# Chunk products of an mLSTM as three products of high and low parts, split by three engines

## The chip, the cores and the metric

One core of a Trainium2 chip runs the whole kernel. The metric is the device time of one execution in microseconds (us); lower is better. The core has TensorE (PE, matrix products; PEld are its weight loads), VectorE (DVE), ScalarE (ACT), GpSimd (POOL) and SyncE (SP), which issues the transfers. Each takes its own instructions in order and waits on semaphores.

## The reference

A layer over 1024 tokens of width 1024: one wide projection `h @ w_in`, an mLSTM branch, a dilated window attention branch, and an output projection. The change touches the mLSTM branch: 4 heads, head width 256, 8 chunks of 128 tokens (L = 128). For each head and chunk n:

```
C_new = decay * C + einsum('l,lk,lv->kv', w, k_j, v_j)          # the state, 256 x 256
n_new = decay * n + einsum('l,lk->k', w, k_j)
s     = einsum('ld,sd->ls', q, k) * exp(log_d - m_t)            # 128 x 128
num   = inter * einsum('ld,dv->lv', q, C_prev) + einsum('ls,sv->lv', s, v)
den   = inter * (q @ n_prev) + s.sum(-1)
h     = num / maximum(|den|, exp(-m_t))
```

A column of ones appended to v gives n and den in the same products (width VE = 258, two such columns).

## The kernel before, in words

The big projections run on TensorE as a list of products by Strassen-like blocks. One product (a **step**, numbered k) is 12 matmuls of 128 x 512: four k-tiles times three passes, (high weight, high data), (high weight, low data), (low weight, high data), all in the type fp32r, in which one matmul is one pass. The high part is a copy rounded to fp32r, the low part is what is left. For the weights of step k+3 ScalarE makes the high part at its step k (L1456, `high`, which waits until product k-1 is done, so that a ring place is free), and then GpSimd (L1080) or, for the products called P7 and P3, VectorE (L1887) subtracts it to get the low part (`low`). GpSimd also makes the weight sums S1 and S2 (L1068, L1074) once in seven steps, S2 after a `low` of VectorE.

Everything else is side work, written into lists per step: `items[k]` are done by TensorE ahead of product k and by the other engines at their step k; `act_late`, `dve_late`, `pool_late`, `sp_late` come last in an engine's step k. In its step GpSimd first makes `low(k+3)` (if it is its own), then the sums, then `pool_late`. ScalarE takes results out, then `high(k+3)`, then `act_late`.

The 32 chunks (c = 8h + n) are placed by hand in `start_of`: head 0 starts at steps 177, 180, 183, 186, 190, 193, 196, 199, head 1 from 203 and head 2 from 238 with 4 or 5 steps between chunks, head 3 at 273, 276, 280, 283, 287, 290, 294, 297.

- `start` at step s: TensorE makes the scores (L1317) and turns o, k and v (L1321, L1332, L1334). ScalarE copies v and scaled k out of PSUM (L1721, L1723), takes the exponential (L1726) and the output gate (L1730). VectorE makes `w` = scores x exponentials (L2165).
- `end` at step s+2: TensorE makes A = q x state (L1345, two matmuls 128 x 258, none for n = 0), B = w x v (L1350, one), C = k x v (L1354, two, none for n = 7), all in fp32 (four passes, which the profile shows as two records for each matmul). ScalarE copies B (L1738), VectorE adds A (L2172), divides, and brings the state up to date (L2190).
- The square of the chunk's output (L1656) is at ScalarE's step s+3. SyncE fetches chunk c+2 into the buffer of chunk c (`chunk_in`) at the step of `end` of c.

VectorE also has the taps of the convolution in head 0 to 2's stretch (L2001, 128 x 1021 to 1023, both inputs in SBUF), one at one step and two at the next, and the silu after them (L2011).

Of the kernel before, what the change touches and what calls it, by code (L numbers as in the profile page):

```python
# [13 lines left out]
P = 128  # L14
# [27 lines left out]
HM_SLOTS = 12  # L42
# [103 lines left out]
def hybrid_kernel(nc, x, w_in, w_if, w_pm, w_pa, w_out, b_gate, conv_wt, conv_bt, pre_wt, m_wt, post_w,  # L146
# [240 lines left out]
    def chunk_no(h, n):  # L387
        return NT * h + n
# [10 lines left out]
    with ctx:  # L399
# [65 lines left out]
        hm_sb = at("hm_sb", [P, HM_SLOTS, MD], F32, A_Q)  # L465
# [15 lines left out]
        sq_junk = small("sq_junk", [P, MD], BF16, 2)  # L481
# [47 lines left out]
        ifw = small("ifw", [P, KT, 2 * MH], F32)  # L529
        assert pos[0] <= nc.sbuf_usable_end, (pos[0], nc.sbuf_usable_end)  # L530
# [51 lines left out]
        x2_in = [sem(f"x2_in{i}") for i in range(4)]  # L582
# [9 lines left out]
        x_sq = sem("x_sq")  # L592
# [13 lines left out]
        e_done, kv_done, sq_done = sem("e_done"), sem("kv_done"), sem("sq_done")  # L606
        m_norm = sem("m_norm")
        att_hi, hm_hi, w_out_hi = sem("att_hi"), sem("hm_hi"), sem("w_out_hi")
        ysq_done, mg_hi = sem("ysq_done"), sem("mg_hi")

        v_step = sem("v_step")
        x_ms, x_sq_late, x_scaled = sem("x_ms"), sem("x_sq_late"), sem("x_scaled")
# [11 lines left out]
        d_done, s34_done, lo_dve = sem("d_done"), sem("s34_done"), sem("lo_dve")  # L624
        a_used, chunk_ready, ones_done = sem("a_used"), sem("chunk_ready"), sem("ones_done")
        m_ms, m_fac = sem("m_ms"), sem("m_fac")
# [3 lines left out]
        y_ms, y_read, y_done = sem("y_ms"), sem("y_read"), sem("y_done")  # L630

        g_ready = sem("g_ready")
        x_rs, x_norm = sem("x_rs"), sem("x_norm")
        s12_done = sem("s12_done")
        lo_pool = sem("lo_pool")
        m_rs, y_rs = sem("m_rs"), sem("y_rs")
# [1674 lines left out]
```

## Time and profile before

| | |
|---|---|
| median of 3 runs | 1371.04 us (1370.8 to 1371.63) |
| the profiled execution, its time | 1369.94 us |
| its span from first to last instruction | 1368.1 us |
| mean granted TensorE clock | 0.998 |
| busy share PE, PEld, DVE, ACT, POOL | 99%, 82%, 58%, 47%, 42% |

The span is what the views of the trace divide up; the profiled execution's time lies 1.84 us above it, and 1.10 us below the median of the runs.

### The profile page before, as it was taken

Reading aid. Unit: us, or ns where it says so; the run is one execution under the profiler, and the core shown is the slowest. Engines: PE = TensorE matmul, PEld = TensorE weight load, DVE = VectorE, ACT = ScalarE, POOL = GpSimd, SP = SyncE. Lnnn points to the kernel's source line nnn. Section 1 sums busy time; section 2 is a strip of 40 time slices with the busy share of each in tenths; the row PEclk is TensorE's granted clock in tenths of the full one; section 3 lists DMA queues with packets and bytes.
Section 4 is the critical chain, followed back from the end, with each engine's and each line's share of the span. In section 5 each row is a group of like instructions: output and inputs, shape, how many; then the busy total and the mean of one; then the engine's idle time right before and its main releaser. Section 6 shows DMA issues by size and latency. Waiting matters only on the chain.

```text
span 1368.1 us, 18779 instructions
## 1 busy us (share of the span) xinstructions
PE 1352.3 (99%) x6470; PEld 1127.3 (82%) x6470; DVE 794.5 (58%) x1260; ACT 641.7 (47%) x1320; POOL 569.2 (42%) x400
## 2 busy tenths in 40 slices
PE   7999999999999999999999999999999999999998
PEld 5788888888888888888888888888888888888786
DVE  5874438346543835877756575755644442997632
ACT  6644543543444455345445445544544553533421
POOL 5253435335443534654434445344333544454000
PEclk9999999999999999999999999999999999999999
DMA  6132233324233323455442634345343354966421
GB/s 194 51 76 65 69 74 90 96 48 126 76 85 72 84 79 61 149 173 144 114 145 66 188 104 134 100 127 175 87 150 97 93 188 165 345 200 196 183 97 58
DMA packets 210462, 165.02 MB, mean 121 GB/s; under 512 B 32400, under 2 KB 186544, under 8 KB 210368
## 3 DMA queue, kind: packets, MB, share of 16 engines
q1 hardware_dynamic: 210224, 163.75, 40.5%
q8 instruction: 53, 0.87, 0.3%
q14 instruction: 41, 0.34, 0.1%
q10 hardware_dynamic: 144, 0.07, 0.0%
HBM read 117.41 MB, written 40.08 MB: 115 GB/s over the span
## 4 chain that ended last, share of the span: by engine, by line
PE 91%; DVE 4%; issue 2%; ACT 1%; DMA 1%; SPq 1%; POOL 0%; DVEq 0%; POOLq 0%; ACTq 0%
PE proj L1244 69%; PE side L1189 3%; PE proj L1189 2%; PE side L1289 2%; PE side L1268 2%; PE side L1345 2%; PE side L1354 2%; PE proj L1170 2%; PE side L1170 2%; PE side L1277 1%; PE side L1317 1%; PE side L1350 1%; PE side L1300 1%; DMA x_sb<-x_in 1%; PE side L1362 1%
## 5 line engine op out<-in xcount | busy, mean ns | idle before, releaser
L1080 POOL TENSOR_TENSOR w_lo<-raw,w_hi 128x512 fp32r<-128x512 f32 x161 | 234.5, 1458 | 413.8 <-ACT w_hi L1456 413.7
L1244 PE MATMUL proj<-hi_T,w_hi 128*128 128x512 f32 x832 | 338.1, 406 | 2.2 <-ACT snap L1474 1.6
L1244 PE MATMUL proj<-hi_T,w_lo 128*128 128x512 f32 x832 | 325.2, 391 | 0.0
L1244 PE MATMUL proj<-lo_T,w_hi 128*128 128x512 f32 x832 | 324.1, 390 | 0.0
L1244 PE MATMUL proj<-hi_B,w_hi 128*128 128x512 f32 x624 | 254.1, 407 | 5.6 <-ACT b_sb L1518 4.0
L1244 PE MATMUL proj<-hi_B,w_lo 128*128 128x512 f32 x624 | 244.2, 391 | 0.0
L1244 PE MATMUL proj<-lo_B,w_hi 128*128 128x512 f32 x624 | 243.6, 390 | 0.0
L1080 POOL TENSOR_TENSOR w_lo<-s_sb,w_hi 128x512 fp32r<-128x512 f32 x104 | 156.7, 1510 | 153.5 <-ACT w_hi L1456 153.4
L1244 PEld LDWEIGHTS proj<-hi_T,w_hi 128*128 128x128 f32 x832 | 156.4, 188 | 36.0 <-issue 3.5
L1244 PEld LDWEIGHTS proj<-hi_T,w_lo 128*128 128x128 f32 x832 | 156.1, 188 | 34.2
L1244 PEld LDWEIGHTS proj<-lo_T,w_hi 128*128 128x128 f32 x832 | 156.6, 188 | 30.4
L1456 ACT ACTIVATE w_hi<-raw 128x512 fp32r<-128x512 f32 x216 | 135.2, 627 | 70.5 <-PE proj L1244 57.6
L1244 PEld LDWEIGHTS proj<-hi_B,w_hi 128*128 128x128 f32 x624 | 117.7, 189 | 29.9 <-ACT b_sb L1518 4.2
L1244 PEld LDWEIGHTS proj<-hi_B,w_lo 128*128 128x128 f32 x624 | 117.4, 188 | 25.4
L1244 PEld LDWEIGHTS proj<-lo_B,w_hi 128*128 128x128 f32 x624 | 117.8, 189 | 22.8
L1074 POOL TENSOR_TENSOR s_sb<-s_sb,raw 128x512 f32<-128x512 f32 x52 | 82.9, 1594 | 91.3 <-DVE w_lo L1887 90.5
L1456 ACT ACTIVATE w_hi<-s_sb 128x512 fp32r<-128x512 f32 x156 | 97.7, 627 | 37.9 <-PE proj L1244 28.9
L1887 DVE TENSOR_TENSOR w_lo<-s_sb,w_hi 128x512 fp32r<-128x512 f32 x52 | 43.9, 845 | 85.5 <-ACT w_hi L1456 85.5
L1068 POOL TENSOR_TENSOR s_sb<-raw 128x512 f32<-128x512 f32 x52 | 75.5, 1453 | 21.5 <-DVE w_lo L1887 21.4
L2001 DVE SCALAR_TENSOR_TENSOR tmp<-stage,cw,tmp 128x1023 f32<-128x1023 f32 (+2 forms) x48 | 76.1, 1585 | 0.7
L2144 DVE CUSTOM_DVE_ANT_0 prob<-side,mask_sb 128x128 f32<-128x128 f32 (+1 forms) x96 | 29.2, 347 | 67.3 <-PE side L1268 67.2
L1474 ACT ACTIVATE snap<-proj 128x512 f32<-128x512 f32 x52 | 31.1, 597 | 78.0 <-PE proj L1244 77.9
(253 smaller groups left out, 2014.5 us busy)
## 6 DMA issues: line engine op xcount, KB each, us to landing
raw<-w_in SPq DMA_DIRECT2D x95, 512.0 KB, 6.0
m_spill<-stage SPq DMA_DIRECT2D x16, 1024.0 KB, 5.6
chunk<-m_spill SPq DMA_DIRECT2D x32, 512.0 KB, 3.8
gate_spill<-stage SPq DMA_DIRECT2D x8, 1024.0 KB, 4.3
gst<-gate_spill SPq DMA_DIRECT2D x32, 256.0 KB, 3.2
share<-share_spill SPq DMA_DIRECT2D x12, 512.0 KB, 5.0
x_sb<-x_in SPq DMA_DIRECT2D x8, 512.0 KB, 7.6
hm_spill<-stage SPq DMA_DIRECT2D x4, 1024.0 KB, 8.8
```

Of the source, the lines that this page charges most:

```text
L1068: ins = TT(s1_sb[:], a21, a22, ALU.add)
L1074: ins = TT(s2_sb[:], s1_sb[:], a11, ALU.subtract)
L1080: TT(w_lo_ring[k % RING][:], src, w_hi_ring[k % RING][:].bitcast(F32), ALU.subtract).then_inc(lo_pool, 1)
L1170: mm = pe.matmul(pa_slot(t)[:, tokens], w[:, kt, :], m[:, kt, tokens], start=(kt == 0 and w is wh and m is at_hi), stop=(kt == AH - 1 and ...
L1189: mm = pe.matmul(y_slot(t)[:, columns], a[:, kt, :], w[i][:, j, columns], start=(kt == 0 and a is hi_part and w is out_hi), stop=(kt == KT ...
L1244: mm = pe.matmul(acc(p, which), w[:, kt, :], m[:, kt, :], start=(first and kt == 0 and w is wh and m is h_hi[b]), stop=(kt == 3 and w is w ...
L1268: mm = pe.matmul(b[:, at_ * P:(at_ + m) * P], qo_sb[(NG * h + g) % 4][:, n * P:(n + 1) * P], k_sb[g][:, (n + 1 - m) * P:(n + 1) * P], star ...
L1456: A(w_hi_ring[k % RING][:], src, ACT.Copy).then_inc(hi_done, 1)
L1474: A(snap[0][:], a, ACT.Copy).then_inc(u3_done, 1)
L1887: TT(w_lo_ring[k % RING][:], operand(p, weight_name(k)), w_hi_ring[k % RING][:].bitcast(F32), ALU.subtract).then_inc(lo_dve, 1)
L2001: ins = STT(t_[:, d:], src[:, 0:S - d], cw[:, t, 3 - d:4 - d], t_[:, d:], ALU.mult, ALU.add)
L2144: ins = V.tensor_tensor_reduce(out=prob_part(h, i)[:, part], in0=b[:, part], in1=mask, scale=-ASCALE, scalar=3.0e38, op0=ALU.add, op1=ALU. ...
```

## The change

All of A, B and C go from fp32 to three fp32r products of high and low parts; the scores stay fp32. The parts are made so:

- q: high by ScalarE as the first thing of `start` (128 x 256), low by GpSimd in `pool_late[s]` (in place over q in the chunk's buffer, so it also waits until the scores are made).
- k, v: high by ScalarE (the two copies that were there, with fp32r outputs), low by VectorE, two more operations that read PSUM (128 x 256 each), between `dmat` and `w`.
- w: VectorE writes it over the exponentials, ScalarE makes the high part in `act_late[s+1]` (128 x 128), GpSimd the low part in `pool_late[s+1]`.
- state: high by ScalarE in `act_late[e+1]`, low by GpSimd in `pool_late[e+1]` (128 x 516 each), e being the step of `end`.

`end` is at e = s+2 where the next chunk starts by s+3 (head 0: n = 0, 1, 2, 4, 5, 6; head 3: n = 0, 2, 4, 6) and at e = s+3 elsewhere. Single buffers take the place of double ones for k, v, w and the output gate; the outputs' ring has 10 places for 12; some semaphores are merged to make room.

```diff
-HM_SLOTS = 12
+HM_SLOTS = 10
...
+    end_of = {}
+    for c, at_ in enumerate(chunks):
+        s = start_of[at_]
+        end_of[at_] = s + (2 if c + 1 < len(chunks) and start_of[chunks[c + 1]] <= s + 3 else 3)
     for h, n in chunks:
-        s = start_of[h, n]
+        s, e = start_of[h, n], end_of[h, n]
         c = NT * h + n
         ready = 7 * pair_of["mo", h] + (10 if h else 11)
-        free = start_of[chunks[c - 2]] + 2 if c > 1 else 171
+        free = end_of[chunks[c - 2]] if c > 1 else 171
         sp_late[max(free, ready)].append(("chunk_in", h, n))
         items[s].append(("start", h, n))
-        items[s + 2].append(("end", h, n))
-        act_late[s + 3].append(("square", h, n))
+        items[e].append(("end", h, n))
+        act_late[s + 1].append(("w_high", h, n))
+        if n:
+            pool_late[s].append(("q_low", h, n))
+        pool_late[s + 1].append(("w_low", h, n))
+        act_late[e + 1].append(("square", h, n))
+        if n < NT - 1:
+            act_late[e + 1].append(("state_high", h, n))
+            pool_late[e + 1].append(("state", h, n))
...
         state = small("state", [P, 2, VE], F32)
-        kw_sb = [small(f"kw{i}", [P, MD], F32) for i in range(2)]
-        vv_sb = [small(f"vv{i}", [P, VE], F32) for i in range(2)]
-        w_sb = [small(f"w{i}", [P, P], F32) for i in range(2)]
-        o_gate = [small(f"o_gate{i}", [P, MD], F32) for i in range(2)]
-        dmat = small("dmat", [P, P], F32)
+        state_hi = small("state_hi", [P, 2, VE], F32R)
+        state_lo = at("state_lo", [P, 2, VE], F32R, A_P + 26112)
+        q_hi = small("q_hi", [P, 2, P], F32R)
+        q_lo = [at(f"q_lo{i}", [P, 2, P], F32R, A_P + 16896 + i * 4608) for i in range(2)]
+        kw_hi, kw_lo = small("kw_hi", [P, MD], F32R), small("kw_lo", [P, MD], F32R)
+        vv_hi, vv_lo = small("vv_hi", [P, VE], F32R), small("vv_lo", [P, VE], F32R)
+        cw_hi, cw_lo = small("cw_hi", [P, P], F32R), small("cw_lo", [P, P], F32R)
+        o_gate = small("o_gate", [P, MD], F32)
+        dmat = at("dmat", [P, P], F32, A_P + 26112 + 2112)
...
+                    if what == "q_low":
+                        h, n = it[1:]
+                        c = chunk_no(h, n)
+                        g.wait_ge(q_high, later_no(h, n))
+                        g.wait_ge(pe_ring, ring_no["qk", h, n] + 1)
+                        TT(q_lo[c % 2][:], chunk_sb[c % 2][:, 0:2, :], q_hi[:].bitcast(F32), ALU.subtract
+                           ).then_inc(q_low, 1)
+                    elif what == "w_low":
+                        h, n = it[1:]
+                        g.wait_ge(w_high, chunk_no(h, n) + 1)
+                        TT(cw_lo[:], dmat[:], cw_hi[:].bitcast(F32), ALU.subtract).then_inc(w_done, 1)
+                    elif what == "state":
+                        h, n = it[1:]
+                        g.wait_ge(state_high, (NT - 1) * h + n + 1)
+                        TT(state_lo[:], state[:], state_hi[:].bitcast(F32), ALU.subtract).then_inc(state_done, 1)
...
+            def three_products(into, w, m):
+
+                for i, (a, b) in enumerate(((0, 0), (0, 1), (1, 0))):
+                    mm = pe.matmul(into, w[a], m[b], start=(i == 0), stop=(i == 2))
+                return mm
+
             def chunk_end(h, n):
                 c = chunk_no(h, n)
-                v = vv_sb[c % 2][:]
+                v = (vv_hi[:], vv_lo[:])
                 pe.wait_ge(kv_done, c + 1)
                 pe.wait_ge(ones_done, 1)
                 if n:
-                    ring_taken(pe, ("C", h, n - 1, 1))
+                    pe.wait_ge(q_low, later_no(h, n))
+                    pe.wait_ge(state_done, later_no(h, n))
                     for d in range(2):
-                        mm = pe.matmul(keep[:, 0:VE], chunk_sb[c % 2][:, d, :], state[:, d, :],
-                                       start=(d == 0), stop=(d == 1))
+                        for a, m in ((q_hi, state_hi), (q_hi, state_lo), (q_lo[c % 2], state_hi)):
+                            mm = pe.matmul(keep[:, 0:VE], a[:, d, :], m[:, d, :],
+                                           start=(d == 0 and a is q_hi and m is state_hi), stop=(d == 1 and a is not q_hi))
                     mm.then_inc(pe_keep, 1)
-                ring_taken(pe, ("qk", h, n))
+                pe.wait_ge(w_done, c + 1)
                 b = work(("B", h, n))
-                pe.matmul(b[:, 0:VE], w_sb[c % 2][:], v, start=True, stop=True).then_inc(pe_ring, 1)
+                three_products(b[:, 0:VE], (cw_hi[:], cw_lo[:]), v).then_inc(pe_ring, 1)
                 if n < NT - 1:
                     for d in range(2):
                         b = work(("C", h, n, d))
-                        pe.matmul(b[:, 0:VE], kw_sb[c % 2][:, d * P:(d + 1) * P], v, start=True, stop=True
-                                  ).then_inc(pe_ring, 1)
+                        keys = slice(d * P, (d + 1) * P)
+                        three_products(b[:, 0:VE], (kw_hi[:, keys], kw_lo[:, keys]), v).then_inc(pe_ring, 1)
...
+                elif what == "w_high":
+                    h, n = it[1:]
+                    c = chunk_no(h, n)
+                    ring_taken(act, ("qk", h, n))
+                    if c:
+                        act.wait_ge(pe_ring, ring_no["B", *divmod(c - 1, NT)] + 1)
+                    A(cw_hi[:], dmat[:], ACT.Copy).then_inc(w_high, 1)
+                elif what == "state_high":
+                    h, n = it[1:]
+                    ring_taken(act, ("C", h, n, 1))
+                    if n:
+                        act.wait_ge(pe_keep, keep_no["A", h, n] + 1)
+                    elif h:
+                        act.wait_ge(pe_keep, keep_no["A", h - 1, NT - 1] + 1)
+                    A(state_hi[:], state[:], ACT.Copy).then_inc(state_high, 1)
...
+                        if n:
+
+                            if later_no(h, n) > 1:
+                                hp, n2 = (h, n - 1) if n > 1 else (h - 1, NT - 1)
+                                act.wait_ge(pe_keep, keep_no["A", hp, n2] + 1)
+                            act.wait_ge(chunk_in[c % 2], 32 * (c // 2 + 1))
+                            A(q_hi[:], chunk_sb[c % 2][:, 0:2, :], ACT.Copy).then_inc(q_high, 1)
                         act.wait_ge(pe_keep, keep_no["kv", h, n] + 1)
-                        if c > 1:
-                            act.wait_ge(pe_ring, ring_no[last_use(*divmod(c - 2, NT))] + 1)
-                        ins = A(vv_sb[c % 2][:, 0:MD], keep[:, MD:2 * MD], ACT.Copy)
+                        if c:
+                            act.wait_ge(pe_ring, ring_no[last_use(*divmod(c - 1, NT))] + 1)
+                        ins = A(vv_hi[:, 0:MD], keep[:, MD:2 * MD], ACT.Copy)
                         if n < NT - 1:
-                            ins = A(kw_sb[c % 2][:], keep[:, 0:MD], ACT.Copy, scale=cols[:, 2, h, n:n + 1])
-                        ins.then_inc(kv_done, 1)
+                            ins = A(kw_hi[:], keep[:, 0:MD], ACT.Copy, scale=cols[:, 2, h, n:n + 1])
+                        ins.then_inc(kv_hi, 1)
                         act.wait_ge(d_done, c + 1)
                         A(dmat[:], dmat[:], ACT.Exp, bias=cols[:, 0, h, n:n + 1]).then_inc(e_done, 1)
                         act.wait_ge(pe_ring, ring_no["oT", h, n] + 1)
-                        if c > 1:
-                            act.wait_ge(chunk_ready, c - 1)
-                        A(o_gate[c % 2][:], bank[ring_no["oT", h, n] % BANKS][:, 0:MD], ACT.Tanh, scale=0.5
+                        if c:
+                            act.wait_ge(chunk_ready, c)
+                        A(o_gate[:], bank[ring_no["oT", h, n] % BANKS][:, 0:MD], ACT.Tanh, scale=0.5
                           ).then_inc(ring_act, 1)
...
+                dve.wait_ge(kv_hi, c + 1)
+                ins = TT(vv_lo[:, 0:MD], keep[:, MD:2 * MD], vv_hi[:, 0:MD].bitcast(F32), ALU.subtract)
+                if n < NT - 1:
+                    ins = STT(kw_lo[:], keep[:, 0:MD], cols[:, 2, h, n:n + 1], kw_hi[:].bitcast(F32), ALU.mult, ALU.subtract)
+                ins.then_inc(kv_done, 1)
                 i = ring_no["qk", h, n]
                 dve.wait_ge(pe_ring, i + 1)
-                if c > 1:
-                    dve.wait_ge(pe_ring, ring_no["B", (c - 2) // NT, (c - 2) % NT] + 1)
                 dve.wait_ge(e_done, c + 1)
-                TT(w_sb[c % 2][:], bank[i % BANKS][:, 0:P], dmat[:], ALU.mult).then_inc(ring_dve, 1)
+                TT(dmat[:], bank[i % BANKS][:, 0:P], dmat[:], ALU.mult).then_inc(ring_dve, 1)
...
+                    if chunk_no(h, n) - h:
+                        dve.wait_ge(state_done, chunk_no(h, n) - h)
```

## Rows read from the trace of the kernel before

**Rows 1.** One window: PE, PEld, DVE, ACT, POOL busy; clock; DMA share; GB/s

```profile
612.00:700.00 88.00, 88.00 (x430) 74.52 (x429) 62.45 (x105) 44.04 (x96) 35.56 (x24) 1.00 0.43 126
```

**Rows 2.** Groups of PE by form: times records, busy us, mean ns

```profile
L1244 PE MATMUL proj<-hi_T,w_lo 128*128 128x512 f32 x832 | 325.2, 391 | 0.0
...
L1354 PE MATMUL side<-vv,kw 128*128 128x258 f32 x112 | 28.9, 381 | 0.0
L1345 PE MATMUL side<-state,chunk 128*128 128x258 f32 x112 | 28.9, 379 | 0.0
...
L1350 PE MATMUL side<-vv,w 128*128 128x258 f32 x64 | 19.1, 379 | 0.0
```

**Rows 3.** The chain in order of time: start, us, what

```profile
619.84 0.43 PE side L1350 x2
...
623.89 0.44 PE side L1317 x4
...
624.99 5.47 PE proj L1244 x24
630.46 0.87 PE side L1345 x4
631.33 0.43 PE side L1350 x2
```

**Rows 4.** Weight loads: scores (ns min/median/max), projection (busy, mean ns, idle)

```profile
L1317 PEld LDWEIGHTS side<-chunk x128: 187/190/192, 612.9 to 1042.4; 128*128 128x128 f32 x128
...
L1244 PEld LDWEIGHTS proj<-hi_T,w_lo 128*128 128x128 f32 x832 | 156.1, 188 | 34.2
```

**Rows 5.** Groups by form of POOL, ACT and DVE

```profile
L1080 POOL TENSOR_TENSOR w_lo<-raw,w_hi 128x512 fp32r<-128x512 f32 x161 | 234.5, 1458 | 413.8 <-ACT w_hi L1456 413.7
...
L1456 ACT ACTIVATE w_hi<-raw 128x512 fp32r<-128x512 f32 x72 | 45.2, 628 | 19.2 <-PE proj L1244 19.2
...
L1721 ACT ACTIVATE vv<-side 128x256 f32<-128x256 f32 x32 | 12.3, 384 | 34.2 <-PE side L1334 34.2
...
L2172 DVE SCALAR_TENSOR_TENSOR total<-side,cols,total 128x258 f32<-128x258 f32 x28 | 13.6, 485 | 26.1 <-ACT total L1738 25.8
```

**Rows 6.** Timeline of POOL: start, us, what [idle before it]

```profile
616.40 4.09 POOL L1080 TENSOR_TENSOR w_lo<-raw,w_hi 128x512 fp32r<-128x512 f32 x2 [6.04 <-ACT w_hi L1456]
...
627.63 1.87 POOL L1080 TENSOR_TENSOR w_lo<-raw,w_hi 128x512 fp32r<-128x512 f32 x1 [2.06 <-ACT w_hi L1456]
629.46 2.25 POOL L1080 TENSOR_TENSOR w_lo<-s_sb,w_hi 128x512 fp32r<-128x512 f32 x1
...
665.80 1.39 POOL L1080 TENSOR_TENSOR w_lo<-raw,w_hi 128x512 fp32r<-128x512 f32 x1 [4.85 <-ACT w_hi L1456]
...
678.61 1.72 POOL L1080 TENSOR_TENSOR w_lo<-raw,w_hi 128x512 fp32r<-128x512 f32 x1
...
688.05 1.30 POOL L1080 TENSOR_TENSOR w_lo<-s_sb,w_hi 128x512 fp32r<-128x512 f32 x1 [5.21 <-ACT w_hi L1456]
...
1008.15 1.29 POOL L1080 TENSOR_TENSOR w_lo<-s_sb,w_hi 128x512 fp32r<-128x512 f32 x1 [3.24 <-ACT w_hi L1456]
```

**Rows 7.** Timeline of DVE and ACT beside it

```profile
627.07 5.72 DVE L2001 SCALAR_TENSOR_TENSOR tmp<-stage,cw,tmp 128x1023 f32<-128x1023 f32 x3
...
663.48 0.64 ACT L1456 ACTIVATE w_hi<-raw 128x512 fp32r<-128x512 f32 x1
```

**Rows 8.** The chain where PE reaches the ends of later chunks

```profile
667.72 0.87 PE side L1345 x4
...
679.23 0.87 PE side L1345 x4
...
690.74 0.87 PE side L1345 x4
...
1011.68 0.87 PE side L1345 x4
```

**Rows 9.** DMA issues of the page: KB each, us to landing

```profile
chunk<-m_spill SPq DMA_DIRECT2D x32, 512.0 KB, 3.8
```

More of the change, by code:

```diff
@@ L581, in hybrid_kernel @@
         out_in = [sem(f"out_in{i}") for i in range(4)]
-        x2_in = [sem(f"x2_in{i}") for i in range(4)]
         y_out = [sem(f"y_out{i}") for i in range(4)]
@@ L590, in hybrid_kernel @@
         pe_y = sem("pe_y")
-        x_sq = sem("x_sq")
+        row_sq = sem("row_sq")
         b1_hi = sem("b1_hi")
@@ L1127, in _ @@
                     what = it[0]
-                    if what == "norm":
+                    if what == "q_low":
[13 more added lines that the diff above has]
+                        TT(state_lo[:], state[:], state_hi[:].bitcast(F32), ALU.subtract).then_inc(state_done, 1)
+                    elif what == "norm":
                         h = it[1]
-                        g.wait_ge(m_ms, h + 1)
-                        TT(mrs[:], msq[:, h % 2], halfneg[:], ALU.pow).then_inc(m_rs, 1)
+                        g.wait_ge(mean_sq, MS_M + h + 1)
+                        TT(mrs[:], msq[:, h % 2], halfneg[:], ALU.pow).then_inc(root, 1)
             for t in range(NT):
-                g.wait_ge(y_ms, t + 1)
-                TT(yrs[:, t:t + 1], ysum[:, t:t + 1], halfneg[:, 0:1], ALU.pow).then_inc(y_rs, 1)
+                g.wait_ge(mean_sq, MS_Y + t + 1)
+                TT(yrs[:, t:t + 1], ysum[:, t:t + 1], halfneg[:, 0:1], ALU.pow).then_inc(root, 1)
         @block.tensor
@@ L1499, in y_squares @@
                 if t or half:
-                    act.wait_ge(ysq_done, 2 * t + half)
+                    act.wait_ge(row_sq, SQ_Y + 2 * t + half)
                 A(y_junk[:], y_slot(t)[:, half_of(half)], ACT.Square, scale=DM ** -0.5,
-                  accum_out=ysq[:, t, half:half + 1]).then_inc(ysq_done, 1)
+                  accum_out=ysq[:, t, half:half + 1]).then_inc(row_sq, 1)
             def square(t):
@@ L2020, in piece @@
                         dve.wait_ge(sq_done, NT * (h + 1))
-                        TS(msq[:, h % 2], msq[:, h % 2], 1.0 / MD, 4.0 * EPS, ALU.mult, ALU.add).then_inc(m_ms, 1)
+                        TS(msq[:, h % 2], msq[:, h % 2], 1.0 / MD, 4.0 * EPS, ALU.mult, ALU.add).then_inc(mean_sq, 1)
                     else:
-                        dve.wait_ge(m_rs, h + 1)
+                        dve.wait_ge(root, ROOT_M + h + 1)
                         TT(mfac[:], mrs[:], rden[:, h % 2], ALU.mult).then_inc(m_fac, 1)
@@ L2039, in mean_square @@
             def mean_square(t):
-                dve.wait_ge(x_sq, t + 1)
-                TS(ssq[:, t:t + 1], ssq[:, t:t + 1], EPS, None, ALU.add).then_inc(x_ms, 1)
+                dve.wait_ge(row_sq, t + 1)
+                TS(ssq[:, t:t + 1], ssq[:, t:t + 1], EPS, None, ALU.add).then_inc(mean_sq, 1)
             def first_low(kt):
@@ L2182, in chunk_end @@
                     dve.wait_ge(pe_ring, ring_no["hmT", hp, 2 + n2 // 4] + 1)
-                STT(hm_slot(h, n), o_gate[c % 2][:], 1.0, total[:, 0:MD], ALU.add, ALU.mult).then_inc(chunk_ready, 1)
+                STT(hm_slot(h, n), o_gate[:], 1.0, total[:, 0:MD], ALU.add, ALU.mult).then_inc(chunk_ready, 1)
                 if n < NT - 1:
+                    if chunk_no(h, n) - h:
+                        dve.wait_ge(state_done, chunk_no(h, n) - h)
                     for d in range(2):
@@ L2231, in result @@
                     columns = half_of(half)
-                    dve.wait_ge(ysq_done, 2 * t + half + 1)
+                    dve.wait_ge(row_sq, SQ_Y + 2 * t + half + 1)
                     if half:
-                        STT(ysum[:, t:t + 1], ysq[:, t, 0:1], EPS, ysq[:, t, 1:2], ALU.add, ALU.add).then_inc(y_ms, 1)
+                        STT(ysum[:, t:t + 1], ysq[:, t, 0:1], EPS, ysq[:, t, 1:2], ALU.add, ALU.add).then_inc(mean_sq, 1)
                     elif t == 0:
@@ L2241, in result @@
                 dve.wait_ge(y_read, 2 * t + 2)
-                dve.wait_ge(y_rs, t + 1)
-                dve.wait_ge(x2_in[t % 4], 16 * (t // 4 + 1))
+                dve.wait_ge(root, ROOT_Y + t + 1)
+                dve.wait_ge(x_in[t], 32)
                 parts = [slice(0, DM)] if t < NT - 1 else [half_of(0), half_of(1)]
```

41 lines of the change are left out of this document (22 added, 19 removed).

## The prediction

> **What bounds the kernel now.** I read first the windows over the stretch of the chunks. From 612 to 700 us TensorE is busy for 88.00 of 88.00 us at a granted clock of 1.00, its higher level of 2.4 GHz, while GpSimd is busy for 35.56 us [rows 1]. The chain that ended last says the same: in this stretch it is TensorE's own instructions, one behind the other [rows 3]. So each microsecond taken off TensorE in it is a microsecond off the time, and each microsecond that TensorE newly waits is one on top; there is no slack to spend. The groups by form then give what is replaced, the chain its pace, and the timelines of GpSimd, VectorE and ScalarE show how early the inputs of `end` could be ready.
>
> **What TensorE saves.** The groups hold 112 records for C, 112 for A and 64 for B [rows 2], two for each matmul: 56 + 56 + 32 = 144 matmuls of 128 x 258. In the chain two of them take 0.87 us [rows 3], 0.435 us each, 62.6 us in all. Each becomes three matmuls of one pass, a form that the trace does not have at this width. Bounds from the nearest rows:
> - From below: a record of the scores is two passes over 128 columns with a weight load of its own, and four of them take 0.44 us [rows 3], 0.110 us. So a weight load and 256 column-times fit into 0.110 us, and the loads of fp32 and of the fp32r products have the same 188 to 190 ns [rows 4]. 258 columns in one pass then take no less than 0.110: 144 x (0.435 - 0.330) = 15.1 us saved.
> - From above: 24 fp32r matmuls of 512 columns take 5.47 us [rows 3], 0.228 each, where 512 columns at 2.4 GHz are 0.213 and the fp32 record of 2 x 258 columns, 0.2175, lies only 0.0025 over its 0.215. fp32r has some 0.0125 us more. If that is a fixed price, a matmul takes 0.1225: 144 x (0.435 - 0.3675) = 9.7 us.
> - If it goes with the columns, 0.0025 stays and the rest of 0.228 is scaled: 0.0025 + 258/512 x 0.2255 = 0.116, so 144 x (0.435 - 0.348) = 12.5 us. I take this one, between the two.
>
> The Trainium skill (TensorE: Matmul & The Clock Gate, section Back-to-back issue gap) has N/2.4 + 2.5 ns for a matmul at the high clock, 110 ns here, by which the saving would be 15.1 us. For 512 columns it gives 216 ns where this trace has 228, so I don't go by it.
>
> **What is added to the others.** GpSimd: a low part of 512 columns takes 1.29 to 1.30 us alone [rows 6] and 1.46 in the mean [rows 5]. By columns the state's low part is 1.30, the queries' 0.65 and w's 0.35 (estimates), up to 2.30 us per chunk, some 66 us in all. GpSimd's 35.56 busy us of 88 [rows 1] have room for it; the order is the question. ScalarE: a 512 copy is 0.63 and a 256 one 0.38 [rows 5], so q's high part 0.38, w's about 0.3, state's 0.63: 1.3 us per chunk, in an engine half idle; q's comes while it waited for `start` anyway. VectorE: two reads of PSUM of 256 columns, about 0.43 each by half to all of the 0.485 for 258 columns [rows 5]: 0.86 us, between `dmat` and `w`, of which about half falls into its wait for ScalarE's exponential (an estimate). Were that cover gone, it would be 0.86 later with its taps; products wait for VectorE's results only two steps (5.5 us) later. The fetch of chunk c+2, moved with `end`, has three or more steps (over 8 us) to land in 3.8 [rows 9]: no price; SyncE's queue behind it waits for nothing new but `end` itself. Merged semaphores, the ring of 10 and single buffers: their last users are a step or more before, no price. Where `end` moves to s+3 the same work stands one product later: nothing.
>
> **Where TensorE will wait.** `end` needs the low parts of q and state (for A) and of w (for B), all from GpSimd, which serves strictly in order: at step s low(s+3), state, q; at step s+1 low(s+4), w. TensorE needs them after `start` and two products, 6.57 us after s. A itself takes six passes, 0.70 us, before w is needed. In the six tight chunks of head 0 that is not enough. I add to the end of GpSimd's last old instruction what now stands in its queue:
> - chunk 0 (no A): GpSimd ended both lows at 620.49 [rows 6], w's part ends at 620.84, B was due at 619.84 [rows 3]: 1.0 us.
> - chunk 1: the second low ended at 631.71 [rows 6]; with 1.30 + 0.65 + 0.35 it is 634.0; B was due at 630.46 [rows 3] + 0.70 = 631.16: 2.85 us.
> - chunk 4 (and chunk 2, with the same distances): ScalarE's high part ends at 664.12 [rows 7], then square and the state's high part until 665.3; 1.30 + 0.65 + 1.29 + 0.35 give 668.9, B due at 667.72 [rows 8] + 0.70: 0.5 us each.
> - chunk 5: low(197), behind the sums, ended at 680.33 [rows 6]; 682.63 against 679.23 [rows 8] + 0.70: 2.7 us.
> - chunk 6: low(199) ended at 689.35 [rows 6], then 1.95 until q's part, against A at 690.74 [rows 8]: 0.6 us.
>
> That is 8.2 us, the lower end. It leaves out what VectorE does to GpSimd. Alone a low takes 1.29; beside three taps of VectorE the two lows took 1.87 and 2.25, and the three taps, back to back in VectorE's program, 5.72 us [rows 6, 7]. The 1.54 us that GpSimd lost and the ends of both fit only one order: tap, low, tap, low, tap, each about 1.1 us and each alone. So an added GpSimd instruction beside an operation of VectorE that reads two SBUF tiles lets one such operation in ahead of it. Replayed so: chunk 1 runs low 628.6 to 629.9, tap, state 631.0 to 632.3, tap, q until 634.1, low 635.4, w 635.8: A waits 3.6 and B 0.9 more, 4.5 us. Likewise chunk 4 gets two taps more (3.6), chunk 5 one tap and a sum (4.2), chunk 6 a sum of 0.6, a low and the silu (2.7), chunk 2 a silu (1.2), chunk 0 sometimes a tap (1.4). Sum 17.6 us.
>
> The Trainium skill (SBUF — State Buffer, section Who interferes with whom) says that a VectorE instruction with two SBUF inputs and a GpSimd instruction that reads SBUF exclude each other for the whole instruction, in order of issue. Were it only the mean of the lows, 1.46 for 1.29, the added queue would wait 13% longer and the stalls stay near 10 us; by the rule they are near the 17.6. The pair 1.87 and 2.25 is on its side.
>
> Elsewhere there is little: in head 3 VectorE has no taps, low(290) ends at 1009.44 [rows 6], state, q and w need 2.30, and A comes at 1011.68 [rows 8]; nothing to 0.3. With `end` at s+3 GpSimd has 2.75 us more. Only where the two sums (2.6 us) fall in between as well (chunk 1 of heads 1 and 2) up to 0.8 us each. I take 0.5 us for all of these, bounds 0 and 1.6.
>
> **Sum.** -12.5 + 17.6 + 0.5 = +5.6 us: 1369.94 would become 1375.5 in the profiled execution, and on the median of the runs, 1371.04 + 5.6 = 1376.6 us. A measurement of this kernel can tell about 0.2%, 2.7 us.
>
> **Rivals.**
> 1. Faster: VectorE and GpSimd hardly block each other, as GpSimd takes its turns in the silent places of VectorE. For it: the lows of 1.29 outside the taps [rows 6]. Against: the pair in chunk 1. Stalls 8.2, saving 12.5 to 15.1: 1371.04 less 4.3 to 6.9, so 1364 to 1367. It decides when the stalls are under 12.5 - 2.7 = 9.8 us.
> 2. The waits spread: ScalarE, which gates GpSimd's lows, is itself late (it waits in order for B, for the taps and for the gate's buffer, now single), and chunks at s+3 wait too. At 0.5 us in each of 20 other chunks that is 10 us more: 1387.
> 3. The change doesn't do what it says: narrow one-pass matmuls don't run at their width. If each took the 0.228 of a 512 one, 144 x (0.684 - 0.435) = 36 us come on top, 1425 with the stalls; at 0.145 nothing is saved, 1389. Against it the 0.110 of the scores' records.
>
> **Chances.** Forecast's case 0.56 (in it 0.40 slower, 0.16 within 0.2%, for its stalls of 13 to 20 us and saving of 9.7 to 15.1 make 1369 to 1382); rival 1 0.27 (0.20 faster, 0.07 same); rival 2 0.11; rival 3 0.06. Faster 0.20, same 0.23, slower 0.57. The range from 1364 (8.2 us of stalls against 15.1) to 1385 leaves out most of rivals 2 and 3 and a little of rival 1.
>
> **What the profile after would show.** Records of A, B, C 432 in number, 0.33 to 0.37 us of the chain for three; TensorE idle for the first time between 612 and 700 us, most of it released by GpSimd's low parts of q, state and w, in head 0's chunks 1, 4, 5 and 6, none in head 3; the state's low part about 1.3 us alone and above 2 beside taps; TensorE's side work shorter by 12.5 us. Wrong makes me: GpSimd's narrow operations cheaper or dearer than their columns, an order of turns other than one by one, or a pace of the narrow matmuls off 0.116.

## The result, and the profile after

The changed kernel takes 1396.42 us in the median of 4 runs (1394.99 to 1397.56), the kernel before 1370.92 beside it (4 runs, 1369.49 to 1371.63): 1.0188 times as long, interval 1.0176 to 1.0200, or 25.5 us slower. Slower was the forecast, 1376.6 us was not: the time lies outside the range of 1364 to 1385. The profiled execution took 1396.55 us; its span is 1394.7 us where before it was 1368.1, and its mean granted clock 0.991 where it was 0.998.

The busy times on the page of the changed kernel, engine by engine (us, share of the span, instructions):

```profile
PE 1356.0 (97%) x6614; PEld 1131.7 (81%) x6614; DVE 835.7 (60%) x1320; ACT 671.5 (48%) x1408; POOL 671.9 (48%) x488
```

No share looks alarming. The window over the first 88 us of the chunks, in the columns of [rows 1], does:

```profile
612.00:700.00 88.00, 75.41 (x370) 62.95 (x369) 54.94 (x95) 40.96 (x93) 48.08 (x35) 0.92 0.37 103
```

TensorE, which had no idle time here, now idles for 12.59 us, and its clock is 0.92 of full speed. The waits of TensorE (what for, us in total, times, longest) name the cause of the idle time:

```profile
PE side L1377 <- POOL cw_lo L1160: 13.0, 14, 1.7
PE side L1390 <- POOL q_lo L1155: 8.7, 8, 3.3
PE proj L1281 <- ACT b_sb L1563: 5.0, 1, 5.0
```

The first two are new, 21.7 us in 22 places; the third is a wait near the kernel's start (at 18 us), 4.0 us long before. It changes from kernel to kernel (2.8 to 5.4 us in those below), which the comparisons of spans carry with them. Where in chunks 1, 4 and 5 of head 0 they fall, TensorE's timeline shows (start, us, what, idle before it):

```profile
633.05 0.39 PE L1281 MATMUL proj<-hi_T,w_lo 128*128 128x512 f32 x1
636.74 0.36 PE L1390 MATMUL side<-state_hi,q_hi 128*128 128x258 f32 x1 [3.30 <-POOL q_lo L1155]
638.18 0.39 PE L1377 MATMUL side<-vv_hi,cw_hi 128*128 128x258 f32 x1 [0.49 <-POOL cw_lo L1160]
...
678.16 0.36 PE L1390 MATMUL side<-state_hi,q_hi 128*128 128x258 f32 x1 [1.41 <-POOL q_lo L1155]
680.58 0.58 PE L1377 MATMUL side<-vv_hi,cw_hi 128*128 128x258 f32 x1 [1.45 <-POOL cw_lo L1160]
...
696.02 0.36 PE L1390 MATMUL side<-state_hi,q_hi 128*128 128x258 f32 x1 [2.04 <-POOL q_lo L1155]
698.43 0.58 PE L1377 MATMUL side<-vv_hi,cw_hi 128*128 128x258 f32 x1 [1.38 <-POOL cw_lo L1160]
```

The same 128 x 258 matmul is written with 0.39 us at 638.18 and with 0.58 at 680.58 and 698.43. That is the clock. Windows of TensorE alone (us, PE busy, PEclk, DMA share, GB/s), first three short ones at the waits, then three of 25 us that hold them:

```profile
638.00:642.00 4.00, 3.81 (x15) 0.59 0.51 150
680.00:686.00 6.00, 5.42 (x17) 0.50 0.35 98
697.00:703.00 6.00, 4.62 (x16) 0.50 0.34 98
625.00:650.00 25.00, 21.21 (x103) 0.93 0.36 97
675.00:700.00 25.00, 18.72 (x82) 0.80 0.31 83
700.00:725.00 25.00, 24.54 (x119) 0.93 0.37 122
```

In each of the three places the granted clock is at its lower level of 1.2 GHz (0.50) for 3 to 7 us. It does not fall at the same point of each: at 638.8 us, 0.6 us after the second wait of chunk 1; at 679.7, inside the second wait of chunk 4; and at 696.8, after the 2.04 us ahead of chunk 5's A and before the wait for w began. Before, this stretch ran at 1.00 [rows 1]. The three windows of 25 us give 25 x (0.07 + 0.20 + 0.07) = 8.5 us of lost clock, but in chunks 4 and 5 a part of it passed while TensorE stood idle. What was lost in work is read from the starts of the matmuls (the first two follow each other at the lower clock, 0.43 us apart, the last two at the higher, 0.25 apart; a narrow product takes 0.215 and not 0.12):

```profile
685.66 0.63 PE L1281 MATMUL proj<-lo_T,w_hi 128*128 128x512 f32 x1
686.09 0.60 PE L1281 MATMUL proj<-hi_T,w_lo 128*128 128x512 f32 x1
686.52 0.41 PE L1281 MATMUL proj<-hi_T,w_hi 128*128 128x512 f32 x1
686.77 0.40 PE L1281 MATMUL proj<-lo_T,w_hi 128*128 128x512 f32 x1
```

Over the three places the matmuls at the lower clock take 6.6 us more than at the higher: 4.3 in 22 projection products, 2.0 in 21 narrow ones, 0.3 in the two first ones behind a wait.

GpSimd's added work, by form (columns as in [rows 5]), is dearer than forecast:

```profile
L1164 POOL TENSOR_TENSOR state_lo<-state,state_hi 128x516 fp32r<-128x516 f32 x28 | 41.3, 1473 | 23.4 <-ACT state_hi L1709 23.4
L1155 POOL TENSOR_TENSOR q_lo<-chunk,q_hi 128x256 fp32r<-128x256 f32 x28 | 35.7, 1275 | 0.0
L1160 POOL TENSOR_TENSOR cw_lo<-dmat,cw_hi 128x128 fp32r<-128x128 f32 x32 | 22.1, 691 | 1.5 <-ACT cw_hi L1701 1.5
```

They take 99.1 us in all, where 66 were estimated; the queries' part has a mean of 1.28 us and not 0.65, w's 0.69 and not 0.35. A little of it is the narrow operations themselves: the shortest take 0.73 and 0.44 us. Chunk 1 shows where the most comes from. GpSimd's timeline there:

```profile
630.65 1.96 POOL L1102 TENSOR_TENSOR w_lo<-raw,w_hi 128x512 fp32r<-128x512 f32 x1 [2.06 <-ACT w_hi L1501]
632.57 2.25 POOL L1164 TENSOR_TENSOR state_lo<-state,state_hi 128x516 fp32r<-128x516 f32 x1
634.78 1.70 POOL L1155 TENSOR_TENSOR q_lo<-chunk,q_hi 128x256 fp32r<-128x256 f32 x1
636.45 1.27 POOL L1102 TENSOR_TENSOR w_lo<-s_sb,w_hi 128x512 fp32r<-128x512 f32 x1
637.68 0.45 POOL L1160 TENSOR_TENSOR cw_lo<-dmat,cw_hi 128x128 fp32r<-128x128 f32 x1
...
827.00 1.96 POOL L1102 TENSOR_TENSOR w_lo<-raw,w_hi 128x512 fp32r<-128x512 f32 x1 [2.06 <-ACT w_hi L1501]
828.92 1.73 POOL L1155 TENSOR_TENSOR q_lo<-chunk,q_hi 128x256 fp32r<-128x256 f32 x1
830.61 2.26 POOL L1102 TENSOR_TENSOR w_lo<-s_sb,w_hi 128x512 fp32r<-128x512 f32 x1
832.82 0.45 POOL L1160 TENSOR_TENSOR cw_lo<-dmat,cw_hi 128x128 fp32r<-128x128 f32 x1
```

and VectorE's beside its first three lines:

```profile
630.18 5.71 DVE L2068 SCALAR_TENSOR_TENSOR tmp<-stage,cw,tmp 128x1023 f32<-128x1023 f32 x3
```

While the three taps run, each GpSimd instruction is longer than alone, by 0.69, 0.95 and 0.97 us: 1.96, 2.25 and 1.70 us for a weight's low part, the state's and the queries', which take 1.27, 1.30 and 0.73 where no tap runs. Once they are over, the next weight's low part takes 1.27 and w's 0.45 us. In a queue served in order the wait of A ends with `q_lo` (634.78 + 1.70 = 636.48, A goes on at 636.74) and that of B with `cw_lo`, which stands behind a weight's low part that nobody needs for three steps. The last four lines are chunk 6 of head 1, whose `end` had been moved to s+3: the same queue, again beside three taps, and B waits 1.48 us there too.

The taps are not the only such operations of VectorE. In head 3, which has none, GpSimd's narrow parts are stretched too, beside VectorE's weight sum and weight low part (0.68 us alone):

```profile
1060.58 1.67 DVE L1948 TENSOR_TENSOR s_sb<-raw,s_sb 128x512 f32<-128x512 f32 x1
1062.17 1.22 DVE L1954 TENSOR_TENSOR w_lo<-raw,w_hi 128x512 fp32r<-128x512 f32 x1
...
1061.67 1.18 POOL L1155 TENSOR_TENSOR q_lo<-chunk,q_hi 128x256 fp32r<-128x256 f32 x1
1062.81 0.91 POOL L1160 TENSOR_TENSOR cw_lo<-dmat,cw_hi 128x128 fp32r<-128x128 f32 x1
```

### The profile page after: what moved, and what is told of

It reads as the page before. It is cut to its first block and busy times, and to the rows that moved or that the text cites. A ratio compares the mean times of both kernels' runs of the same rounds, so it can differ in the third digit from the quotient of the medians.

```text
span 1394.7 us, 19471 instructions
## 1 busy us (share of the span) xinstructions
PE 1356.0 (97%) x6614; PEld 1131.7 (81%) x6614; DVE 835.7 (60%) x1320; ACT 671.5 (48%) x1408; POOL 671.9 (48%) x488
## 5 line engine op out<-in xcount | busy, mean ns | idle before, releaser
L1102 POOL TENSOR_TENSOR w_lo<-raw,w_hi 128x512 fp32r<-128x512 f32 x161 | 242.9, 1510 | 337.5 <-ACT w_hi L1501 337.5
L2068 DVE SCALAR_TENSOR_TENSOR tmp<-stage,cw,tmp 128x1023 f32<-128x1023 f32 (+2 forms) x48 | 81.0, 1688 | 0.7
```

The costliest lines, as they stand in the source:

```text
L1102: TT(w_lo_ring[k % RING][:], src, w_hi_ring[k % RING][:].bitcast(F32), ALU.subtract).then_inc(lo_pool, 1)
L2068: ins = STT(t_[:, d:], src[:, 0:S - d], cw[:, t, 3 - d:4 - d], t_[:, d:], ALU.mult, ALU.add)
```

## The experiments

Each was run beside the kernel before on the same chip. In all of them `before` is its median there, and the ratio has its interval.

**Is the clock a cost of its own?** TensorE is given dummy products in the three places where the clock fell, so that it is busy while it would wait; nothing that the waits depend on is changed.

```diff
+FILL = {1: 27, 4: 12, 5: 17}
+FILL_B = {1: 4, 4: 12, 5: 12}
...
+                    for _ in range(FILL.get(c, 0)):
+                        pe.matmul(keep[:, 0:VE], h_hi["B11"][:, 0, 0:P], h_hi["B11"][:, 0, 0:VE], start=True, stop=True)
...
+                for _ in range(FILL_B.get(c, 0)):
+                    pe.matmul(b[:, 0:VE], h_hi["B11"][:, 0, 0:P], h_hi["B11"][:, 0, 0:VE], start=True, stop=True)
                 pe.wait_ge(w_done, c + 1)
```

> The changed kernel with dummy products of 128 x 258 on TensorE where it waits longest: 27, 12 and 17 ahead of A of chunks 1, 4 and 5 and 4, 12 and 12 ahead of their B, about as long as the waits that they fill, into PSUM that is overwritten right after. Theory C (a part of the loss is the clock, which fell to the lower level for 16.8 us after these waits): granted clock 1.00 in the three places, and the time falls by 8.4 us to about 1388 (1386 to 1390), although nothing is taken away. If the lower clock costs nothing, or falls anyway: 1396 to 1399.

Measured: 1392.01 us against 1371.39 before, 1.0152 [1.0136, 1.0167]; span 1387.9, clock 0.998. Windows of TensorE in the three places, columns as above:

```profile
634.00:642.00 8.00, 7.81 (x50) 1.00 0.26 77
674.00:684.00 10.00, 9.80 (x64) 1.00 0.20 61
689.00:699.00 10.00, 9.80 (x64) 1.00 0.31 89
```

The clock stays at its higher level, and the kernel with more work in it is, by the two ratios, 0.0036 shorter, some 5 us in the median; the profiled run, the fastest of its four, is 6.8 us shorter in the span, 1.4 of it in the wait near the start (3.6 for 5.0 us). The theory that the fall of the clock costs time of its own stands. The 8.4 us that were expected did not all come back: the wait ahead of chunk 6's A grew from 0.46 to 1.86 us, and 1392 is 4 above what was expected. The clock is worth some 5 to 7 us, which fits the 6.6 read from the starts.

**Is it the order in GpSimd's queue?** In every step the chunk's low parts go ahead of the weights' low part and the sums, and ScalarE's high parts of w and state ahead of what else it has in that step. The work is the same.

```diff
-                if k and k + LEAD < NK and not low_dve[k + LEAD]:
-                    low(k + LEAD)
-                if k in sums_at:
-                    add(sums_at[k], "S1")
-                    add(sums_at[k], "S2")
                 for it in pool_late[k]:
...
+                if k and k + LEAD < NK and not low_dve[k + LEAD]:
+                    low(k + LEAD)
+                if k in sums_at:
+                    add(sums_at[k], "S1")
+                    add(sums_at[k], "S2")
```

> The changed kernel with the chunk's high parts of w and state ahead of the rest of ScalarE's step, and the chunk's low parts ahead of the weights' low part and the sums in GpSimd's step. Same instructions, another order. If the waits come from the order of GpSimd's queue (theory A): the low parts are ready one to three us before they are needed, TensorE's waits on GpSimd fall from 21.7 us to under 4, the clock stays at its higher level in the whole chunk stretch, and the time is 1371 less about 10.8 us of shorter products plus what is left of waits: 1359 to 1366. If GpSimd and VectorE are out of room in head 0 because they exclude each other (theory B): the same work is still in the way, half the waits stay: 1376 to 1388.

Measured: 1373.39 us against 1371.39, 1.0015 [1.0006, 1.0024]; span 1371.8. The order alone takes back 23 of the 25.5 us. TensorE's waits of this kernel:

```profile
PE side L1365 <- DVE state L2273: 6.6, 5, 2.1
...
PE side L1384 <- POOL cw_lo L1157: 3.6, 4, 1.2
```

What was 21.7 us is 3.6, and from 612 to 700 us the clock is 1.00. It still came out above what the theory of the order alone expected, since a wait appeared that neither theory had: 6.6 us in five places in which `start`'s transposes wait for VectorE's update of the state. Of the largest, VectorE's timeline shows

```profile
762.85 3.50 DVE L2079 SCALAR_TENSOR_TENSOR tmp<-stage,cw,tmp 128x1022 f32<-128x1022 f32 x2
...
769.01 2.32 DVE L2089 SCALAR_TENSOR_TENSOR stage<-stage,tmp 128x1024 f32<-128x1024 f32 x1
...
773.39 0.87 DVE L2273 SCALAR_TENSOR_TENSOR state<-state,decay,side 128x258 f32<-128x258 f32 x2
```

The VectorE operations that read two SBUF tiles are stretched (the last takes 1.22 us elsewhere), and the state's update behind them comes late. That it is GpSimd's low parts that stretch them is shown by the run below with the same order and narrow low parts: there this wait is gone. Put GpSimd's urgent work ahead, and it is VectorE that pays. Behind the largest of these waits, 2.12 us, the clock fell as well, to 0.73 from 775 to 780 us.

**Is it the exclusion?** The three taps are cut to two columns each, so VectorE holds GpSimd up for next to nothing; the order is as in the changed kernel.

```diff
-                        ins = STT(t_[:, d:], src[:, 0:S - d], cw[:, t, 3 - d:4 - d], t_[:, d:], ALU.mult, ALU.add)
+                        ins = STT(t_[:, d:d + 2], src[:, 0:2], cw[:, t, 3 - d:4 - d], t_[:, d:d + 2], ALU.mult, ALU.add)
```

> The changed kernel with VectorE's taps of the convolution cut to 2 columns each (the output is not the reference's), all else in its place. It takes away the operations of two SBUF inputs that GpSimd's stand against, and leaves the order of GpSimd's queue. If the exclusion makes most of the waits (theory B): the state's low part 1.3 us and q's 0.7 everywhere, waits on GpSimd down to the 8 to 9 us of the bare queue, no fall of the clock, 1370 to 1374. If it is the order alone (theory A): waits of 17 us or more, over 1385.

Measured: 1373.27 us against 1369.92, 1.0027 [1.0015, 1.0038]; span 1371.6, clock 0.998. TensorE's waits:

```profile
PE side L1377 <- POOL cw_lo L1160: 5.1, 10, 1.3
PE side L1390 <- POOL q_lo L1155: 4.5, 6, 2.1
```

9.6 us remain of 21.7, and the clock does not fall. So 12 us of the waits and all of the clock's loss hang on VectorE's taps, and 9.6 us on the rest of the queue. Two things hang on the taps at once, and this run does not part them. GpSimd's own operations get shorter: its three low parts take 84.8 us for 99.1, the weights' 378.9 for 397.5. And ScalarE, whose high parts GpSimd waits for, waits for the taps itself, 28.4 us in the changed kernel and 1.7 here. How much of the 12 us is exclusion and how much a late ScalarE stays open. In chunk 5 the wait ahead of A is as long as in the changed kernel, 2.05 us for 2.04. The mean of `q_lo` is 996 ns here, that of `cw_lo` 603: they are still above 0.65 and 0.35, as VectorE's other operations with two SBUF inputs are left. The Trainium skill (SBUF — State Buffer, section Who interferes with whom) has a VectorE instruction with two SBUF inputs contend with a GpSimd instruction that reads SBUF, and calls the pair of ports that they share an exclusive lock; the timelines above agree, 2.25 us beside the taps for what takes 1.30 alone.

**What does a narrow product take, and what is left without the low parts?** From chunk 1 on the three low parts are made for two columns only, and the queries' high part stands where their low part is multiplied; TensorE has as many products as before. The output is not the reference's. Once in the order of the change, once with the urgent order.

```diff
-                        TT(cw_lo[:], dmat[:], cw_hi[:].bitcast(F32), ALU.subtract).then_inc(w_done, 1)
+                        w_ = 2 if chunk_no(h, n) else P
+                        TT(cw_lo[:, 0:w_], dmat[:, 0:w_], cw_hi[:, 0:w_].bitcast(F32), ALU.subtract).then_inc(w_done, 1)
...
```

> The changed kernel with GpSimd's low parts of q, w and state cut to 2 columns after the first time (TensorE multiplies as many operands as before, q's high part standing in for its low part; the output is not the reference's). It prices TensorE's part of the change alone. With 0.12 us for a narrow fp32r product, 144 x (0.435 - 0.36) = 10.8 us: 1360 (1358 to 1363). At 0.116 us 12.5 us: 1358.5. If the loss were in the products themselves or in the added work of ScalarE and VectorE, it would stay above 1371.

> e1_urgent with GpSimd's low parts cut to 2 columns after the first time, as in e2_no_low (q's high part stands in for its low part; the output is not the reference's). It should leave TensorE's shorter products with hardly a wait. At 0.12 us for a narrow product 1371.4 - 10.8 + 0 to 2 us of waits left at the first chunks: 1360 to 1363. At 0.116 us: 1358.5 to 1361.

Measured: 1369.62 us against 1371.39, 0.9988 [0.9978, 0.9999], and with the urgent order 1361.07 against 1370.07, 0.9933 [0.9918, 0.9948]. The first was expected 10 us lower. TensorE still waits 6.7 us in five places: 4.7 in chunks 0 and 1, where w's and the state's first low parts are whole, and 2.0 in chunks 4 and 5, where GpSimd's low part of w is two columns wide and late by its place in the queue. And from 612 to 700 us the clock is 0.98. In the second 1.5 us of waits are left, the clock is 1.00, and the kernel is 9.0 us faster. Its chain of waits (start, us, what) reads

```profile
667.18 0.73 PE side L1399 x6
667.91 1.07 PE side L1386 x9
```

A is six products in 0.73 us, B and C nine in 1.07: 0.12 us each, where 0.116 was taken. So 144 x (0.435 - 0.36) = 10.8 us are saved and not 12.5; with the 1.5 us of waits that is 9.3, beside 9.0 measured. The Trainium skill (TensorE: Matmul & The Clock Gate, section Back-to-back issue gap) has N/2.4 + 2.5 ns for an isolated matmul at the high clock, 0.110 us at this width, by which 15.1 us would be saved; the trace does not agree, 0.12.

**Is there a version that wins?** A is the product with the most to wait for: two low parts of its own. It goes back to fp32 on `chunk_sb` and `state`, B and C stay in three products; the low parts of the queries and the state go.

```diff
-                        for a, m in ((q_hi, state_hi), (q_hi, state_lo), (q_lo[c % 2], state_hi)):
-                            mm = pe.matmul(keep[:, 0:VE], a[:, d, :], m[:, d, :],
-                                           start=(d == 0 and a is q_hi and m is state_hi), stop=(d == 1 and a is not q_hi))
+                        mm = pe.matmul(keep[:, 0:VE], chunk_sb[c % 2][:, d, :], state[:, d, :],
+                                       start=(d == 0), stop=(d == 1))
...
```

> The changed kernel with A back in fp32 (no parts of q and state); B and C still three products each, so GpSimd has only w's low part left of the added work. Theory A: the wait for q and state goes, w's low part comes some 2 us sooner and is in time nearly everywhere; 88 of the 144 matmuls are cheaper by 0.075 us: 1371 - 6.6 + up to 2 of waits = 1364 to 1367. If w's low part alone were late by the waits seen for it (13 us in 14 places): 1377.

> A in fp32 and B and C as three products, as in e4_a_fp32, with w's high and low part at the head of ScalarE's and GpSimd's step as in e1_urgent. GpSimd has 0.45 us per chunk to do for it. Waits on w's low part under 2.5 us (5.3 without the order), no wait for VectorE, clock at its higher level: 1371.4 - 6.6 + 2 = 1366 to 1368. If VectorE's lateness is what makes the new wait of e1_urgent whatever the state's parts cost: 1371 or more.

Measured: 1372.86 us against 1371.39, 1.0011 [1.0001, 1.0021], in the order of the change, above the 1364 to 1367 that were expected, since w's part still stands behind the weights' (5.3 us in three places) and the clock falls behind one of these waits (0.98 from 612 to 700 us); with the urgent order 1366.81 against 1369.92, 0.9973 [0.9962, 0.9983]. That is the only version with the reference's whole computation that beats the kernel before, by 3.1 us. TensorE's windows of it, the stretch of [rows 1] and the place where the kernel with the urgent order alone had fallen to 0.73:

```profile
612.00:700.00 88.00, 87.15 (x451) 1.00 0.42 125
775.00:780.00 5.00, 5.00 (x28) 1.00 0.92 236
```

It gives up 56 x 0.075 = 4.2 us of the saving and keeps 88 x 0.075 = 6.6; of these 3.1 are seen in the medians. The span of its profiled run is 5.3 us shorter (1368.1 to 1362.8), but that run is the fastest of seven, and 1.2 of the 5.3 are in the wait near the start (2.8 for 4.0 us). Where the rest of the 6.6 stays is open.

**Does another engine do it better?** First the queries' low part alone on VectorE, then all three low parts there, then those with the urgent order on ScalarE.

```diff
-            pool_late[s].append(("q_low", h, n))
-        pool_late[s + 1].append(("w_low", h, n))
+        dve_late[s + 1].append(("w_low", h, n))
...
-            pool_late[e + 1].append(("state", h, n))
+            dve_late[e + 1].append(("state", h, n))
...
```

> The changed kernel with q's low part made by VectorE, right after its product for w, in place of GpSimd in the same step. Theory A (GpSimd's one queue is what is late): 1.2 to 1.7 us less ahead of A and of w in each chunk; TensorE's waits on GpSimd fall from 21.7 us to about 10, the clock falls in at most one place: 1374 to 1380. Theory B (VectorE and GpSimd together have no room beside the taps): the work is still there, only on the other side: 1386 or more.

> The changed kernel with all three low parts (q, w, state) made by VectorE at the same steps, none by GpSimd: about 1.4 us more per chunk on VectorE (0.39 + 0.3 + 0.69), 2.3 to 3.4 us less on GpSimd. Theory A (one queue, each part behind the weights' low part and the sums): the queue is gone, but VectorE's own has the taps, so waits of some 5 to 8 us in head 0, none in head 3: 1366 to 1372. Theory B (VectorE has no room beside the taps): 1378 or more.

> e6_all_dve with ScalarE's high parts of w and state at the head of its step. If ScalarE's place is part of the lateness there: 1 to 4 us faster than e6_all_dve. If VectorE's own work is what is late, the same time within 1.5 us.

Measured: 1383.95 us against 1369.92, 1.0105 [1.0091, 1.0119]; 1374.23 against 1370.07, 1.0027 [1.0015, 1.0039]; 1375.95 against 1370.07, 1.0044 [1.0028, 1.0061]. None is faster. TensorE's waits in the second:

```profile
PE side L1375 <- DVE cw_lo L2093: 6.8, 8, 1.6
PE side L1356 <- DVE state L2272: 5.1, 5, 1.1
```

The waits moved with the work. With the queries' part alone on VectorE, w's part still came late from GpSimd, 14.2 us in ten places, and the clock from 612 to 700 us was 0.92 as in the change, more than the expectation allowed. With all three on VectorE some 12 us of waits are left and the clock does not fall: it has more room for them than GpSimd, but not enough. That this version is 22 us below the change fits VectorE's shorter operations (a low part of 512 columns takes it 0.68 us, GpSimd 1.3); this was not tried apart. The urgent order on ScalarE took 2.4 us off the waits for w's part and brought one of 1.8 us for ScalarE's copy of B; the kernel came out 1.7 us slower, which neither theory had.

**What does moving `end` do?** Once in the kernel before, where all else is kept (the first line of the diff is put in); once the other way round, with the urgent order and every `end` at s+2 again, to take away the wait for the state's update.

```diff
-        end_of[at_] = s + (2 if c + 1 < len(chunks) and start_of[chunks[c + 1]] <= s + 3 else 3)
+        end_of[at_] = s + 2
```

> The kernel before, all in fp32, with only the ends of the chunks moved as in the change: s+2 where the next chunk starts by s+3, s+3 elsewhere. By the prediction the move costs nothing: 1371 (1369 to 1372), no waits of TensorE in the chunk stretch. If the move by itself makes start wait for VectorE's state update, as in e1_urgent (6.6 us in 5 places): 1374 or more.

> e1_urgent with the end of every chunk at s+2, as in the kernel before. In e1_urgent TensorE waited 6.6 us in 5 places of start for VectorE's state update, which stood one product later for the ends at s+3. If that move is the cause, those waits go, the parts are still in time: waits 10.2 to about 4 us, 1371.4 - 10.8 + 4.5 = 1364 to 1367. If VectorE is late by its taps alone, the waits stay, at the end's or the start's place: 1372 or more.

Measured: 1370.89 us against 1370.07, 1.0007 [0.9998, 1.0016]: the move alone costs nothing that shows. And 1377.12 against 1369.92, 1.0049 [1.0035, 1.0063]: the wait for the state's update is gone, as expected, but one product less between `start` and `end` makes w's part late,

```profile
PE side L1384 <- POOL cw_lo L1157: 12.4, 10, 2.0
```

12.4 us instead of 3.6. The step that the change gives `end` is worth more than the wait that it brings; 1364 to 1367 was expected, so I had the larger effect wrong.

## Why the prediction was right in direction and wrong in size

**Right: what bounds it, and that the change would pay with waits.** TensorE had no slack, all of the new waits are for GpSimd's low parts, and with those made nearly free the saving comes out nearly whole (9.0 of 10.8 us).

**Right: the order of turns.** The replay of chunk 1 gave A 3.6 and B 0.9 us of waiting; they are 3.30 and 0.49. The other chunks of head 0, forecast and measured: chunk 0 1.4 and 1.67, chunk 2 1.2 and 0.85, chunk 4 3.6 and 2.86, chunk 5 4.2 and 3.42, chunk 6 2.7 and 0.46. The pattern holds but for chunk 6. The sum is 13.05 us where 17.6 was taken and 8.2 was the lower end: the term was too high by 4.55, so the miss does not lie here; it hides a part of it.

**Wrong: no term for the clock.** This is the first failed step: the prediction let a wait cost what it lasts, the granted clock having been 1.00 [rows 1]. At the waits in chunks 1, 4 and 5 it fell to 0.50, and 6.6 us went with it. The dummy products show that it is a cost of its own (some 5 us back in the median, though the low parts still came late).

**Wrong: "Elsewhere there is little", 0.5 us.** This is the second, and the largest. In heads 1 to 3 TensorE waited 8.65 us in 12 places, nine of them for w's part: 1.48 at 833.33, in a chunk at s+3, and 1.33 at 998.35 in head 3, where none or 0.3 was forecast. In heads 1 and 2 the three taps stretch the queue as in head 0 (the chunk at 827.00 above), and GpSimd first waits 2.06 us for ScalarE's high part, which is rival 2's mechanism beside that of the forecast. Head 3 was argued from state, q and w alone, as VectorE has no taps there. But its weight sums and low parts read two SBUF tiles as well and stretch q's part to 1.18 and w's to 0.91 us; and the weights' low part ahead of w was not replayed. In sum the two terms for waits were 18.1 us against 21.7: an error of 8.15 here was hidden in part by the 4.55 of head 0.

**Mis-sized: the narrow product.** 0.12 us and not 0.116, within the bounds of 0.110 and 0.1225: 10.8 us saved and not 12.5.

**Left out: the two ends of a wait.** A projection's product has a mean of 0.40 us in the records but follows the one before by 0.228. The 0.16 us between them count as busy while TensorE already stands: the product at 633.05 is followed at 636.74, 3.46 us late, where the row has 3.30. Taken from the starts, A and B are late by 26.0 us in all between the first and the last chunk's scores, 4.3 more than the rows of idle time show; 0.7 of these are short waits in four places without a row. And behind a wait the first product takes 0.21 us to the next and not 0.12, in 26 places 2.3 us.

**The sum.** Between those scores are 141 of the 144 matmuls, 10.6 us saved: -10.6 + 21.7 + 4.3 + 2.3 + 6.6 = +24.3 us. Between the first and the last chunk's scores lie 1042.4 - 612.9 = 429.5 us before [rows 4], and in the changed kernel, by the weight loads of the same matmuls,

```profile
L1354 PEld LDWEIGHTS side<-chunk x128: 187/190/192, 614.2 to 1067.9; 128*128 128x128 f32 x128
```

453.7, or 24.2 us more. The rest of the 26.6 of the spans is 1.3 ahead of the stretch, 1.0 of it the longer wait near the start, and 1.1 behind it, 0.9 of it a wait for VectorE that was not there before; neither is explained. Of the 24.2, 19.7 arise before head 1 begins and 4.5 in heads 1 to 3, which waste their saving of some 8 us.

**Right: the prices of nothing.** Moving `end` costs nothing that shows in the kernel before, and no wait is shown for the fetch of a chunk. Not tried was whether the single buffers for v, w and the gate cost something; in the changed kernel they name no wait of TensorE.

## What to carry to other kernels

Where an engine is full, price an edit as what it saves less every wait that it brings, and ask what the clock does at the waits; where the rows of before show no such place, the fall of the clock still gets a term of its own, with a lower end of nothing. In an engine that serves in order, put the short work that the full engine needs next ahead of the long work that has steps to spare: here that alone was worth 23 us, twice what the edit could save. Look for every operation that the other engine's work can stand against, not for the longest alone: in head 3 it was the weight sums, not the taps. And split only those operands whose parts come from an engine with room at that moment: A, with two late low parts, was better left in fp32.

## What the runs showed of the hardware that was not expected

- The granted clock fell at short waits: after 3.30 and 0.49 us, after 1.41 and within the next wait, and after 2.04 us before the next began. It was at 0.50 for 3 to 7 us and came back while TensorE was busy. A single wait of 2.12 us in the kernel with the urgent order was followed by 0.73 from 775 to 780 us. But the length of a wait does not settle it: 2.05 and 0.48 us in the kernel without taps (683.54 and 684.99) left the clock at 1.00 from 683 to 692 us, and so did the single 1.48 us at 833.33 in the changed kernel (833 to 840 us).
- GpSimd's narrow operations do not go by their columns: alone, 128 x 512 takes 1.27 to 1.30 us, 128 x 256 0.73, not 0.65, and 128 x 128, a quarter, 0.45, not 0.33.
- An idle time in a row of TensorE is 0.16 us shorter than the delay that the starts show, and the first product behind it takes 0.21 us to the next and not 0.12.
- An fp32r product of 258 columns takes 0.12 us, one of 512 columns 0.228: half the width is 0.53 of the time.
